# The last feed-forward block's gate and up products as seven block products instead of eight

## The chip, the cores and the metric

The kernel is one program on one core of a Trainium2 chip. The metric is the device time of one execution in microseconds (us), the median over several runs. The engines of the core are TensorE (PE in the rows: matrix products; PEld is its weight load), VectorE (DVE), ScalarE (ACT), GpSimd (POOL) and SyncE (SP), which issues the transfers of the weights.

## The reference

Two models run one after the other on 512 tokens of width 1024: two layers (a gated recurrent mixer, then banded attention, each with a memory attention and a feed-forward block), and a third with differential and forgetting attention. The change concerns the last feed-forward block, with D_MODEL = 1024 and D_FF_2 = 2816 = 22 tiles of 128 columns:

```python
h2 = rmsnorm_2(x, norm2_g[l])
g = jnp.einsum('bsd,df->bsf', h2, w_gate[l])
u = jnp.einsum('bsd,df->bsf', h2, w_up[l])
x = x + jnp.einsum('bsf,fd->bsd', jax.nn.silu(g) * u, w_down[l])
return rmsnorm_2(x, normf_g)
```

Everything is float32. After this block only the final norm is left.

## The kernel before

**Precision.** Each float32 operand of a large product is split in two fp32r parts: a high part (ScalarE copies it to fp32r) and a low part (VectorE subtracts the high one from the original). A product is three matmuls that accumulate in PSUM: high by high, high by low, low by high. Activations lie as [feature, token], so 512 tokens are the moving operand, and the stationary operand is a 128x128 piece of the weights.

**Weights.** All weights lie in the order of use in one array, cut in units of 2048 columns (1 MB; `UNITS`, made by `plan`). SyncE loads unit n into one of two `raw` buffers as soon as the low part of unit n-2 has been made. ScalarE makes `WH` (L1375) and VectorE `WL` (L1806), each in two pieces of 1024 columns, into two double buffers; a new one is begun when TensorE is through with the unit two before.

**One order for all engines.** `order` writes a list of steps; each engine goes through the same list and takes its part of each step, in order, and waits on semaphores. So a conversion that stands in the list behind another step waits for that step's work on the same engine. `conv_ahead` puts the conversions into the list.

**The last feed-forward block.** `ffn` runs two halves (`HALVES`: 12 and 10 of the 22 tiles). Per tile there are 8 K tiles x 3 = 24 matmuls for gate and 24 for up, all 128x128 by 512 tokens (step `fm`, L995). VectorE multiplies the gate by the row factor `Rsb` out of PSUM (L1768), ScalarE takes the silu (L1627), GpSimd multiplies by `Rsb` (L2383), VectorE multiplies by the up product (L2135), ScalarE and GpSimd split the result (L1642, L2391). After each half follow its down products (step `down`, L1299), in banks for four output tiles at a time, and VectorE adds them to X (L2160 and neighbours). The very last output tile is made in two token halves.

**Before the block.** The output projection of the attention makes the 8 tiles of X (L929, steps `out_rest` and `out_all`, tiles 4 to 7 with 24 matmuls each). For each tile the step `res_norm` follows: VectorE adds to X (L2106), ScalarE makes the scaled high part `hH` (L1609) and the square (L1617), VectorE the low part `hL` (L1774), GpSimd adds up the squares (L2374). After two tiles of the block, step `rstd_rows` sums over the partitions (L1080), ScalarE takes the root (L1426) and VectorE the reciprocal (L1842), which gives `Rsb`.

**At the end.** For the last four output tiles VectorE adds to X, ScalarE squares and scales (L1684, L1687), and VectorE adds the square to `acc` (L2171), in that order for each tile. Then the final norm follows.

## Time and profile before

| | us |
|---|---|
| median of 3 runs (lowest to highest) | 1824.84 (1824.78 to 1824.85) |
| profiled execution, span from first to last instruction | 1822.8 |
| a time of its own for the profiled execution, beside its span | none is given; the median of the runs is 2.0 above the span |
| TensorE busy | 1810.1 (99%) |
| TensorE weight loads | 1472.7 (81%) |
| VectorE busy | 938.6 (51%) |
| ScalarE busy | 727.8 (40%) |
| GpSimd busy | 272.3 (15%) |

The busy time of an engine counts every moment in which one of its instructions is open. Matmuls overlap in the pipeline, so the duration of one is longer than its share of the time: the share comes from the time that a row of many takes, divided by their count.

### The profile page before, as it was taken

The numbers are of one execution on the slowest core, as the hardware profiler recorded it, in microseconds if no ns is written. First come the engines' busy times: TensorE is split into PE (matmuls) and PEld (weight loads), VectorE is DVE, ScalarE is ACT, GpSimd is POOL, SyncE is SP. The second block draws the span as 40 slices with busy tenths as digits, with TensorE's granted clock in tenths as the row PEclk, the third lists the DMA queues.
The fourth block names the chain that finished last, engine by engine and source line by source line (L and its number), as shares of the span: only waits on it lengthen the run. The fifth ranks groups of instructions, "written<-read, shape, count | busy, mean of one in ns | idle before, by whom it ended". The sixth has DMA issues, their size and how long they took to land.

```text
span 1822.8 us, 21331 instructions
## 1 busy us (share of the span) xinstructions
PE 1810.1 (99%) x8733; PEld 1472.7 (81%) x8733; DVE 938.6 (51%) x1429; ACT 727.8 (40%) x1155; POOL 272.3 (15%) x241
## 2 busy tenths in 40 slices
PE   9999999999999999999999999999999999999998
PEld 7877788888888887878888888877777888888886
DVE  6878556443453456545653345458667443333324
ACT  5644444331332435654432233332567432212223
POOL 2001222210121200002221022103001222101210
PEclk9999999999999999999999999999999999999999
DMA  6121123222222333212223222232121132222221
GB/s 243 67 88 66 70 95 114 93 93 94 91 95 96 118 128 108 82 47 93 93 95 113 93 93 95 91 110 99 70 103 59 70 109 100 93 92 93 102 89 64
DMA packets 32337, 173.41 MB, mean 95 GB/s; under 512 B 4064, under 2 KB 6240, under 8 KB 14320
## 3 DMA queue, kind: packets, MB, share of 16 engines
q1 hardware_dynamic: 26848, 162.55, 25.0%
q10 hardware_dynamic: 5392, 9.51, 1.6%
q8 instruction: 69, 1.13, 0.2%
q14 instruction: 28, 0.23, 0.0%
HBM read 169.38 MB, written 2.13 MB: 94 GB/s over the span
## 4 chain that ended last, share of the span: by engine, by line
PE 96%; ACT 1%; DVE 1%; DMA 0%; POOL 0%; issue 0%; SPq 0%; ACTq 0%; DVEq 0%; POOLq 0%
PE ps L995 54%; PE ps L1299 20%; PE ps L929 7%; PE ps L1014 5%; PE ps L1141 2%; PE ps L1186 2%; PE ps L1166 2%; PE ps L1034 1%; PE ps L1225 1%; PE ps L1206 1%; DMA raw<-in_wall 0%; ACT PC L1543 0%; DVE WL L1806 0%; ACT WH L1375 0%; POOL sq L2326 0%
## 5 line engine op out<-in xcount | busy, mean ns | idle before, releaser
L995 PE MATMUL ps<-hH,WH 128*128 128x512 f32 x1456 | 570.9, 392 | 0.1
L1806 DVE TENSOR_TENSOR WL<-raw,WH 128x1024 fp32r<-128x1024 f32 (+2 forms) x308 | 377.3, 1264 | 368.1 <-ACT WH L1375 367.9
L995 PE MATMUL ps<-hH,WL 128*128 128x512 f32 x1456 | 566.7, 389 | 0.0
L995 PE MATMUL ps<-hL,WH 128*128 128x512 f32 x1456 | 566.7, 389 | 0.0
L1375 ACT ACTIVATE WH<-raw 128x1024 fp32r<-128x1024 f32 (+2 forms) x308 | 301.4, 1026 | 311.8 <-PE ps L1299 228.6
L995 PEld LDWEIGHTS ps<-hH,WH 128*128 128x128 f32 x1456 | 273.3, 188 | 65.3 <-issue 7.3
L995 PEld LDWEIGHTS ps<-hH,WL 128*128 128x128 f32 x1456 | 273.3, 188 | 57.0
L995 PEld LDWEIGHTS ps<-hL,WH 128*128 128x128 f32 x1456 | 273.3, 188 | 56.9 <-issue 1.0
L1299 PE MATMUL ps<-fL,WH 128*128 128x512 f32 x531 | 205.9, 388 | 0.0
L1299 PE MATMUL ps<-fH,WL 128*128 128x512 f32 x531 | 205.9, 388 | 0.0
L1299 PE MATMUL ps<-fH,WH 128*128 128x512 f32 x531 | 205.9, 388 | 0.0
L2383 POOL TENSOR_TENSOR Y<-Y,Rsb 128x512 f32<-128x512 f32 x66 | 85.2, 1292 | 544.0 <-ACT Y L1632 380.3
L1299 PEld LDWEIGHTS ps<-fH,WH 128*128 128x128 f32 x531 | 99.7, 188 | 20.6
L1299 PEld LDWEIGHTS ps<-fL,WH 128*128 128x128 f32 x531 | 99.7, 188 | 20.5
L1642 ACT ACTIVATE fH<-Z 128x512 fp32r<-128x512 f32 x66 | 41.7, 632 | 186.4 <-DVE Z L2135 186.4
L1299 PEld LDWEIGHTS ps<-fH,WL 128*128 128x128 f32 x531 | 99.7, 188 | 20.3
L2391 POOL TENSOR_TENSOR fL<-Z,fH 128x512 fp32r<-128x512 f32 x66 | 85.2, 1291 | 199.0 <-ACT fH L1642 199.0
L2135 DVE TENSOR_TENSOR Z<-ps,Y 128x512 f32<-128x512 f32 x66 | 45.3, 687 | 113.7 <-PE ps L995 108.9
L1768 DVE TENSOR_TENSOR GG<-ps,Rsb 128x512 f32<-128x512 f32 x66 | 45.4, 690 | 107.6 <-PE ps L995 107.6
L2124 DVE SCALAR_TENSOR_TENSOR Y<-GG,cols,Y 128x511 f32<-128x511 f32 x88 | 67.8, 770 | 40.4 <-ACT Y L1629 38.9
L1629 ACT ACTIVATE Y<-GG,cols 128x512 f32<-128x512 f32 x44 | 35.9, 815 | 111.1 <-DVE GG L1768 111.1
L1014 PE MATMUL ps<-WH,hH 128*128 128x256 f32 x256 | 73.5, 287 | 0.0
(369 smaller groups left out, 2020.7 us busy)
## 6 DMA issues: line engine op xcount, KB each, us to landing
raw<-in_wall SPq DMA_DIRECT2D x140, 1024.0 KB, 4.6
raw<-in_wall SPq DMA_DIRECT2D x12, 768.0 KB, 4.0
bias<-in_bias ACTq DMA_DIRECT2D x12, 256.0 KB, 3.3
X<-in_xt SPq DMA_DIRECT2D x8, 256.0 KB, 8.9
CB<-rows ACTq DMA_DIRECT2D x8, 256.0 KB, 3.3
raw<-in_wall SPq DMA_DIRECT2D x4, 256.0 KB, 5.8
mrA<-in_memt ACTq DMA_DIRECT2D x4, 256.0 KB, 6.3
Mb<-m_rows ACTq DMA_DIRECT2D x4, 256.0 KB, 4.8
```

Of the source, the lines that this page charges most:

```text
L929: mm = e.matmul(ps[b][:, :], ww[:, k, c:c + 128], x, start=(k == seq[0] and i == 0), stop=(k == seq[-1] and i == 2))
L995: mm = e.matmul(ps[b][:, 0:N], ww[:, k, c:c + 128], x[:, k, 0:N], start=(k == 0 and i == 0), stop=(k == 7 and i == 2))
L1014: mm = e.matmul(o, x[:, k, t * 128:t * 128 + 128], ww[:, k, :], start=(k == 0 and i == 0), stop=(k == 7 and i == 2))
L1299: mm = e.matmul(ps[b][:, t], ww[:, kx, mi * 128:mi * 128 + 128], x[:, k, t], start=(gi == first and kx == 0 and p == 0), stop=(gi == end a ...
L1375: e.activation(WH[n % NCV][:, c], raw[n % NRAW][:, c], ACT.Copy).then_inc(*mark("wh", n, x))
L1642: e.activation(F[i]["H"][:, k, :], F[i]["Z"][m % 2][:, :], ACT.Copy).then_inc(*mark("fH", i, int(half), k))
L1768: return e.tensor_tensor(dst, src, Rsb[:, :], ALU.mult)
L1806: e.tensor_tensor(WL[n % NCV][:, c], raw[n % NRAW][:, c], WH[n % NCV][:, c].bitcast(F32), ALU.subtract).then_inc(*mark("wl", n, x))
L2124: e.scalar_tensor_tensor(out=y[:, d:512], in0=gq[:, 0:512 - d], scalar=col(f"fw{i}", c), in1=y[:, d:512], op0=ALU.mult, op1=ALU.add).then_inc(
L2135: e.tensor_tensor(F[i]["Z"][m % 2][:, :], ps[BANK[(name, m)]][:, :], F[i]["Y"][m % 4][:, :], ALU.mult).then_inc(*mark("fz", name, m))
L2383: e.tensor_tensor(y[:, :], y[:, :], Rsb[:, :], ALU.mult).then_inc(*mark("fy", i, m))
L2391: e.tensor_tensor(F[i]["L"][:, k, :], F[i]["Z"][m % 2][:, :], F[i]["H"][:, k, :].bitcast(F32), ALU.subtract).then_inc(*mark("fL", i, int(h ...
```

## The change

The last block's gate and up products become one 2x2 block product, for each of 11 stages s of two gate tiles and two up tiles. The blocks of the weights are (gate, up) by (even K tiles, odd K tiles), 1024 columns each; the blocks of the activations are (even, odd K tiles) by (tokens 0 to 255, 256 to 511). Seven products q1 to q7, each of 4 K tiles x 2 column tiles x 3 = 24 matmuls of 256 tokens, take the place of eight. Their operands:

- Activations: the blocks themselves for q1, q2, q3 (`TH`, `TL`) and four sums for q4 to q7 (`DH`, `DL`). They are made in `res_norm`, for a pair of X tiles at a time, in one scratch tile `Tf`. The next pair's first scaling waits until the low parts of the pair before are done.
- Weights: the unit of conversion is now a chunk of 1024 columns, in one of four slots. For q5, q6, q3 and q7 VectorE first adds two blocks (or a sum and a block) into one of two `Wsum` buffers (step `wsum`); then ScalarE and VectorE convert it as any other (step `cconv`). A third `raw` buffer is used in the block.
- Results: q1, q6, q7, q4 accumulate in one bank, q5 and q3 in a second, q2 in a third. ScalarE copies the intermediate values out (step `wcopy`), VectorE combines them (`wc12`, `wc11`, `wz1`, `wz0`); gate factor, silu and GpSimd's two steps work on 1024 columns for two tiles at once.

The order of the products in a stage is q1, q5, q6, q3, q7, q2, q4, then down products of earlier tiles (24 matmuls of 512 tokens per piece: one piece in stages 1 and 2, two in stages 3 to 10). Stage 0 begins with q1, q5 and q2 over their first three K tiles, then `rstd_rows`, then their fourth. After stage 10 only four tiles of down products are left (`wtail`), so each of the last output tiles ends with 6 matmuls behind the others' where it was 9. The count of down matmuls is 528 before and after. The bytes loaded are the same.

```diff
+WINO = (2,)
+NSU = 11
+CHUNK = 1024
+W_SLOTS = 2 * NCV
...
+def down_pieces(s):
+    if s == 0:
+        return []
+    if s < 3:
+        return [(0, s - 1)]
+    return [((s - 1) // 2, 2 * ((s - 1) % 2) + x) for x in (0, 1)]
...
+def group_tiles(g):
+    return (0, 2) if g == 0 else (4 * g - 2, 4)
...
+def wino_sequence():
+    out = []
+    for s in range(NSU):
+        q = lambda n, p0=0, p1=4, s=s: ("q", s, n, p0, p1)
+        d = [("d",) + x for x in down_pieces(s)]
+        if s == 0:
+            out += [q(1, 0, 3), q(5, 0, 3), q(2, 0, 3), q(1, 3), q(5, 3), q(2, 3), q(6), q(3), q(7),
+                    ("q", 1, 1, 0, 4), q(4)]
+        elif s < 3:
+            out += ([] if s == 1 else [q(1)]) + [q(5), q(6), q(3), q(7), q(2), q(4)] + d
+        else:
+            out += [q(1), q(5), q(6), q(3), q(7), q(2), q(4)] + d
+    return out
...
+                else:
+                    c["sum"] = {5: ((units[0], CHUNK), (units[1], 0)), 6: ((i, "q", s, 5), (units[0], 0)),
+                                3: ((i, "q", s, 6), (units[1], CHUNK)), 7: ((units[0], 0), (units[0], CHUNK))}[q]
+                    c["place"] = {5: 0, 6: 1, 3: 0, 7: 1}[q]
+                c["from"] = units[0] if q == 1 else units[1]
...
     def conv_ahead(end):
-        while now["conv"] < min(end, len(UNITS)) and (now["conv"] < NCV or now["conv"] - NCV in done):
-            for x in (0, 1):
-                put("conv", now["conv"], x)
+        while now["conv"] < len(ITEMS):
+            item = ITEMS[now["conv"]]
+            kind, n = item
+            first = n if kind == "unit" else CHUNKS[n]["from"]
+            if first >= end or any((b if b[0] == "chunk" else b[1]) not in done for b in W_BEFORE[item]):
+                return
+            if kind == "unit":
+                for x in (0, 1):
+                    put("conv", n, x)
+            else:
+                for c in range(now["summed"], min(n + 2, len(CHUNKS))):
+                    if CHUNKS[c]["i"] == CHUNKS[n]["i"]:
+                        if CHUNKS[c]["sum"]:
+                            put("wsum", c)
+                        now["summed"] = c + 1
+                put("cconv", n)
             now["conv"] += 1
...
+        for at, x in enumerate(SEQUENCE):
+            conv_ahead(len(UNITS))
+            if x[0] == "d":
+                _, g, c = x
+                put("wd", i, g, c)
+                while late:
+                    put(*late.pop(0))
+                used((i, "d", g, c))
+                put("wx", i, g, c)
+                continue
+            _, s, q, p0, p1 = x
+            put("wp", i, s, q, p0, p1)
+            while late:
+                put(*late.pop(0))
+            if at == 2:
+                put("rstd_rows", FFN_NORMS[i], 61 if i == 2 else 60)
+            if p1 < 4:
+                continue
+            used((i, "q", s, q))
+            if q in (1, 5, 6, 7):
+                put("wcopy", i, s, q)
+            elif q == 3:
+                put("wc12", i, s)
+            elif q == 2:
+                put("wc11", i, s)
+            if q == (3 if s == 0 else 2):
+                put("wgate", i, s)
+            if q == 4:
+                put("wz1", i, s)
+                late.append(("wz0", i, s))
+        while late:
+            put(*late.pop(0))
+        hread = ("wq", i, NSU - 1, 4)
+        if i == 2:
+            put("sqrt_table")
+        for mg in (0, 1):
+            n = ROLE[i, "T", mg]
+            now["unit"] = n + 1
+            conv_ahead(n + 2)
+            for gi, ks in TAIL:
+                for mi in range(4):
+                    put("wtail", i, mg, gi, mi, n, ks)
+                    if gi == 2:
+                        put("res_ffn", i, 1, 4 * mg + mi, hread)
+            done.add(n)
+        if end:
+            rstd(end, 60)
     def ffn(i, acts, end):
...
+                elif what == "wp":
+                    i, st, pn, p0, p1 = a
+                    c = CHUNK_AT[i, "q", st, pn]
+                    kind = {1: "wA", 6: "wA", 7: "wA", 4: "wA", 5: "wD", 3: "wD", 2: "wB"}[pn]
+                    opens = pn in (1, 5, 2)
+                    if opens and p0 == 0:
+                        b, before = bank((kind, i, st), {"wA": ("wg", "z", 0), "wD": ("wg", "c12"), "wB": ("wg", "c11")}[kind] + (i, st),
+                                         hold=kind == "wA")
+                        if before:
+                            w.wait_ge(*at(*before))
+                    b = BANK[kind, i, st]
+                    if not opens:
+                        w.wait_ge(*at("wcopy", i, st, {6: 1, 7: 6, 4: 7, 3: 5}[pn]))
+                    w.wait_ge(*at("wl", "c", c))
+                    W = [x.rearrange("p (k c) -> p k c", k=4) for x in chunk_slot(c)]
+                    for p in range(p0, p1):
+                        w.wait_ge(*at("wg", "t", "L", i, p, int(pn > 3)))
+                        H, L = moving(pn, p)
+                        for u in (0, 1):
+                            for n, (ww, x) in enumerate(((W[0], H), (W[0], L), (W[1], H))):
+                                mm = e.matmul(ps[b][:, 256 * u:256 * u + 256], ww[:, p, 128 * u:128 * u + 128], x,
+                                              start=(opens and p == 0 and u == 0 and n == 0),
+                                              stop=(p == 3 and u == 1 and n == 2), skip_group_check=True)
+                    if p1 == 4:
+                        mm.then_inc(*mark("wq", i, st, pn))
+                        FREED["chunk", c] = ("wq", i, st, pn)
+                    if pn == 4:
+                        turns.append(b)
...
+                elif what == "wcopy":
+                    i, st, pn = a
+                    dst = {1: held_q1, 5: held_q5, 6: held_v, 7: held_w}[pn]
+                    w.wait_ge(*at("wq", i, st, pn))
+                    if st:
+                        w.wait_ge(*at(*{1: ("wg", "c11"), 5: ("wg", "z", "c22"), 6: ("wg", "c12"), 7: ("wg", "z", 1)}[pn], i, st - 1))
+                    e.activation(dst[:, :, :], by_tile(BANK["wD" if pn == 5 else "wA", i, st]), ACT.Copy).then_inc(
+                        *mark("wcopy", i, st, pn))
...
+                    if st in WINO_OF:
+                        i, p = WINO_OF[st], m // 2
+                        src = X[:, m, :].rearrange("p (h t) -> p h t", h=2)
+                        if p:
+                            w.wait_ge(*at("wg", "t", "L", i, p - 1, 1))
+                        e.activation(Tf[:, 1:3, :] if m % 2 else Tf[:, 0:8:7, :], src, ACT.Copy,
+                                     scale=col(st, m)).then_inc(*mark("wcopy", "t", "g", i, m))
+                        if m % 2:
+                            w.wait_ge(*at("wcopy", "t", "g", i, m))
+                            e.activation(TH[:, p, :, :], Tf[:, 0:3, :], ACT.Copy).then_inc(*mark("wcopy", "t", "H", i, p, 0))
+                            w.wait_ge(*at("wg", "t", "d", i, p, 4))
+                            e.activation(DH[:, p, :, :], Tf[:, 3:7, :], ACT.Copy).then_inc(*mark("wcopy", "t", "H", i, p, 1))
...
+                elif what == "wsum":
+                    c = CHUNKS[a[0]]
+                    src = []
+                    for y in c["sum"]:
+                        if len(y) == 2:
+                            w.wait_ge(*loaded(y[0]))
+                            src.append(raw[RAW_AT[y[0]]][:, y[1]:y[1] + CHUNK])
+                        else:
+                            w.wait_ge(*at("wg", "sum", CHUNK_AT[y]))
+                            src.append(Wsum[CHUNKS[CHUNK_AT[y]]["place"]][:, :])
+                    before = [v for v in range(a[0]) if CHUNKS[v]["sum"] and CHUNKS[v]["place"] == c["place"]]
+                    if before:
+                        w.wait_ge(*at("wl", "c", before[-1]))
+                    e.tensor_tensor(Wsum[c["place"]][:, :], src[0], src[1], ALU.add).then_inc(*mark("wg", "sum", a[0]))
...
+                    if st not in WINO_OF:
+                        low_part(st, m, col(st, m))
+                    elif m % 2:
+                        i, p = WINO_OF[st], m // 2
+                        B12 = Tf[:, 7:8, :].broadcast_to([128, 2, 256])
+                        w.wait_ge(*at("wcopy", "t", "g", i, m))
+                        e.tensor_tensor(Tf[:, 4:7:2, :], Tf[:, 0:3:2, :], B12, ALU.subtract).then_inc(
+                            *mark("wg", "t", "d", i, p, 2))
+                        w.wait_ge(*at("wg", "t", "d", i, p, 2))
+                        e.scalar_tensor_tensor(out=Tf[:, 5, :], in0=Tf[:, 0, :], scalar=-1.0, in1=Tf[:, 6, :],
+                                               op0=ALU.mult, op1=ALU.subtract).then_inc(*mark("wg", "t", "d", i, p, 3))
+                        w.wait_ge(*at("wg", "t", "d", i, p, 3))
+                        e.scalar_tensor_tensor(out=Tf[:, 3, :], in0=Tf[:, 5, :], scalar=-1.0, in1=Tf[:, 1, :],
+                                               op0=ALU.mult, op1=ALU.subtract).then_inc(*mark("wg", "t", "d", i, p, 4))
+                        w.wait_ge(*at("wcopy", "t", "H", i, p, 0))
+                        e.tensor_tensor(TL[:, p, :, :], Tf[:, 0:3, :], TH[:, p, :, :].bitcast(F32),
+                                        ALU.subtract).then_inc(*mark("wg", "t", "L", i, p, 0))
+                        w.wait_ge(*at("wcopy", "t", "H", i, p, 1))
+                        e.tensor_tensor(DL[:, p, :, :], Tf[:, 3:7, :], DH[:, p, :, :].bitcast(F32),
+                                        ALU.subtract).then_inc(*mark("wg", "t", "L", i, p, 1))
...
+                elif what == "wz1":
+                    i, st = a
+                    w.wait_ge(*at("wcopy", i, st, 7))
+                    w.wait_ge(*at("wcopy", i, st, 5))
+                    e.tensor_tensor(held_w[:, :, :], held_w[:, :, :], held_q5[:, :, :], ALU.add).then_inc(
+                        *mark("wg", "z", "c22", i, st))
+                    w.wait_ge(*at("wg", "z", "c22", i, st))
+                    w.wait_ge(*at("wpool", "y", i, st))
+                    e.scalar_tensor_tensor(out=yz[:, :, 256:512], in0=held_w[:, :, :], scalar=-1.0,
+                                           in1=yz[:, :, 256:512], op0=ALU.mult, op1=ALU.mult).then_inc(
+                        *mark("wg", "z", 1, i, st))
+                elif what == "wz0":
+                    i, st = a
+                    w.wait_ge(*at("wq", i, st, 4))
+                    w.wait_ge(*at("wpool", "y", i, st))
+                    e.scalar_tensor_tensor(out=yz[:, :, 0:256], in0=by_tile(BANK["wA", i, st]), scalar=-1.0,
+                                           in1=yz[:, :, 0:256], op0=ALU.mult, op1=ALU.mult).then_inc(
+                        *mark("wg", "z", 0, i, st))
...
+                elif what == "wgate":
+                    i, st = a
+                    R = Rsb[:, :].rearrange("p (o t) -> p o t", o=1).broadcast_to([128, 2, 512])
+                    w.wait_ge(*at("wsilu", i, st))
+                    e.tensor_tensor(yz[:, :, :], yz[:, :, :], R, ALU.mult).then_inc(*mark("wpool", "y", i, st))
+                elif what == "wz0":
+                    i, st = a
+                    f = 2 * st % 8
+                    w.wait_ge(*at("wsilu", "H", i, st))
+                    e.tensor_tensor(FL[:, f:f + 2, :], yz[:, :, :], FH[:, f:f + 2, :].bitcast(F32),
+                                    ALU.subtract).then_inc(*mark("wpool", "L", i, st))
```

## Rows read from the trace of the kernel before

**Rows 1.** The page: busy time per engine (part 1) and the chain's shares (part 4)

```profile
PE 1810.1 (99%) x8733; PEld 1472.7 (81%) x8733; DVE 938.6 (51%) x1429; ACT 727.8 (40%) x1155; POOL 272.3 (15%) x241
...
PE 96%; ACT 1%; DVE 1%; DMA 0%; POOL 0%; issue 0%; SPq 0%; ACTq 0%; DVEq 0%; POOLq 0%
```

**Rows 2.** Windows: stretch, length, busy us (count) by engine, clock, DMA share, GB/s

```profile
1463.00:1582.70 119.70, 119.70 (x530) 99.07 (x529) 47.32 (x46) 37.36 (x47) 29.67 (x23) 1.00 0.27 97
```

**Rows 3.** The chain in order of time, last block: start us, us, what

```profile
1451.26 10.88 PE ps L995 x48
...
1463.00 119.73 PE ps L995 x528
...
1648.01 108.80 PE ps L995 x480
```

**Rows 4.** The same chain, 256-column matmuls of a memory product

```profile
676.20 5.76 PE ps L1014 x48
```

**Rows 5.** Timeline of TensorE, 256-column matmuls with weights stationary: start, us

```profile
12.47 0.28 PE L958 MATMUL ps<-mLA,WH 128*128 128x256 f32 x1
12.58 0.28 PE L958 MATMUL ps<-mHA,WL 128*128 128x256 f32 x1
```

**Rows 6.** VectorE's groups by shape, 1451 to 1823: count, busy us, mean ns, idle before

```profile
L1806 DVE TENSOR_TENSOR WL<-raw,WH 128x1024 fp32r<-128x1024 f32 x58 | 73.3, 1303 | 75.6 <-ACT WH L1375 75.6
...
L2160 DVE TENSOR_TENSOR X<-X,ps 128x512 f32<-128x512 f32 x15 | 10.2, 685 | 12.1 <-PE ps L1299 12.1
...
L1842 DVE RECIPROCAL Rsb<-Rsb 128x512 f32<-128x512 f32 x1 | 3.4, 3353 | 4.7 <-ACT Rsb L1426 4.7
...
L2287 DVE SCALAR_TENSOR_TENSOR X<-X,cols,ps 128x256 f32<-128x256 f32 x2 | 0.9, 471 | 0.0
```

**Rows 7.** ScalarE's groups by shape, the same stretch

```profile
L1375 ACT ACTIVATE WH<-raw 128x1024 fp32r<-128x1024 f32 x58 | 57.9, 1046 | 60.2 <-PE ps L1299 58.6 <-POOL acc L2374 1.6
...
L1609 ACT ACTIVATE hH<-X,cols 128x512 fp32r<-128x512 f32 x2 | 1.4, 724 | 3.3 <-DVE X L2106 3.3
```

**Rows 8.** GpSimd's groups by shape, the same stretch

```profile
L2383 POOL TENSOR_TENSOR Y<-Y,Rsb 128x512 f32<-128x512 f32 x22 | 28.4, 1293 | 163.7 <-ACT Y L1627 163.7
L2374 POOL TENSOR_TENSOR acc<-acc,sq 128x512 f32<-128x512 f32 x2 | 2.7, 1337 | 5.0 <-ACT sq L1617 5.0
```

**Rows 9.** Timeline of VectorE ahead of the block and in it: start, us, idle before

```profile
1430.20 0.68 DVE L2106 TENSOR_TENSOR X<-X,ps 128x512 f32<-128x512 f32 x1
...
1456.67 2.36 DVE L1806 TENSOR_TENSOR WL<-raw,WH 128x1024 fp32r<-128x1024 f32 x2 [2.52 <-ACT WH L1375]
...
1476.31 2.60 DVE L1806 TENSOR_TENSOR WL<-raw,WH 128x1024 fp32r<-128x1024 f32 x2 [1.65 <-ACT WH L1375]
```

**Rows 10.** Timeline of GpSimd beside it

```profile
1475.40 1.29 POOL L2391 TENSOR_TENSOR fL<-Z,fH 128x512 fp32r<-128x512 f32 x1 [0.47 <-ACT fH L1642]
```

**Rows 11.** Timeline of VectorE at 1272 us, then of GpSimd there

```profile
1272.62 3.45 DVE L1806 TENSOR_TENSOR WL<-raw,WH 128x1024 fp32r<-128x1024 f32 x2
```
```profile
1272.13 1.73 POOL L2413 TENSOR_TENSOR dk<-U,RC 128x512 f32<-128x512 f32 x1 [2.15 <-DVE U L1769]
```

**Rows 12.** Windows after TensorE's last matmul: columns as in rows 2

```profile
1816.00:1817.00 1.00, 0.00 (x0) 0.00 (x0) 1.00 (x3) 0.00 (x0) 0.00 (x0) 0.75 1.06 373
1817.00:1818.00 1.00, 0.00 (x0) 0.00 (x0) 1.00 (x2) 0.00 (x0) 0.00 (x0) 0.50 0.59 209
```

**Rows 13.** Timeline of VectorE at the end of the down products

```profile
1805.13 0.69 DVE L2160 TENSOR_TENSOR X<-X,ps 128x512 f32<-128x512 f32 x1 [1.35 <-PE ps L1299]
1806.51 0.69 DVE L2171 TENSOR_TENSOR acc<-acc,sq 128x512 f32<-128x512 f32 x1 [0.70 <-ACT sq L1684]
1807.17 0.69 DVE L2160 TENSOR_TENSOR X<-X,ps 128x512 f32<-128x512 f32 x1
...
1810.69 0.68 DVE L2156 TENSOR_TENSOR acc<-acc,sq 128x512 f32<-128x512 f32 x1
```

**Rows 14.** Transfers issued from 1400 to 1480: count, KB each, us to landing

```profile
raw<-in_wall SPq DMA_DIRECT2D x7, 1024.0 KB, 4.5
```

375 lines of the change are left out of this document (339 added, 36 removed).

## The prediction

> **What bounds the kernel now.** I read the page first: TensorE is busy for 1810.1 of 1822.8 us and makes 96% of the chain that ends last; VectorE is at 51%, ScalarE at 40%, GpSimd at 15% [rows 1]. Then a window of the last block: TensorE has no idle time in 119.70 us while VectorE is busy for 47.32 and GpSimd for 29.67 [rows 2]. So only two things can move the time: what a TensorE instruction costs, and a wait that TensorE does not have today. The price of a matmul comes from the chain, not from the duration of one, since they overlap: 119.73 us for 528 and 108.80 for 480 are 226.7 ns for each matmul of 512 columns, and with the first 48 the gate and up products are 1056 matmuls, 239.4 us [rows 3].
>
> **The matmuls.** The change makes 11 x 7 x 24 = 1848 matmuls of 256 columns of them. A row of 48 such matmuls takes 5.76 us, 120.0 ns each [rows 4], and where the weights are the stationary operand, as here, they start 0.11 to 0.12 us apart [rows 5]. So 221.8 us take the place of 239.4: 17.6 us less. Seven eighths of 239.4 would be 29.9 less; the difference is that 256 columns cost 6.7 ns more than half of 512 (226.7 / 2 = 113.3). The 528 down matmuls stay at 226.7 ns: nothing. The Trainium skill, "TensorE: Matmul & The Clock Gate", section "Back-to-back issue gap", gives an isolated spacing of N / 2.4 + 2.5 ns, 109 and 216; an estimate by it would be 228 - 202 = 26 us saved. The rows do not agree for this data type, and the sum goes by the rows.
>
> **VectorE in a stage.** The extra work is on VectorE. A low part of 1024 columns costs 1.18 us (2.36 for two in a row [rows 9]; the mean duration, 1303 ns, holds waits on ScalarE and contention [rows 6]); the trace has no sum of two weight blocks, but it is an operation of the same kind and size, so I take 1.18 (bounds: that, and the mean of 1.30, 0.5 us a stage more). A stage from the third on has 4 sums and 9 low parts (15.3), the gate factor on 1024 columns (1.2), five combining passes of 512 columns at 0.69 (3.4), and four adds to X at 0.69 (2.8) [rows 6]: 22.7 us. GpSimd's two passes double in width, 2.6 us each by two of 1293 ns [rows 8], and they slow VectorE: two low parts took 2.60 where the GpSimd row overlaps them by 0.38 us, against 2.36, a loss of 0.24 or 0.63 of the overlap [rows 9, 10]; at 1272 us an overlap of 1.24 made them 3.45, a loss of 0.88 of it [rows 11]. So 5.2 us cost 3.3 (up to 4.6), and the stage asks VectorE for 26.0. TensorE takes 7 x 2.88 + 2 x 5.44 = 31.0, so this is hidden, with four converted chunks (8.6 us of products) as the cushion. In stage 0, without down products, it is 20.9 against 20.2, and in stages 1 and 2 24.8 against 25.6: covered by the cushion only. ScalarE has 11 passes of 1024 columns at 1.05 and 4 of 512 at about 0.7, 14 us a stage [rows 7]: nothing. Loads of 1 MB land 4.5 us after their issue [rows 14]. The later of a stage's two units can be issued when q4's low part of the stage before is made, some 9 us after that stage's q1 began, and its first sum stands 17 us after it: over 3 us to spare, nothing; were it gone, VectorE's cushion of 8.6 would still lie before TensorE. The wait of the products on the copies of earlier ones lies one product (2.88 us) behind a copy of 0.7: nothing. The last stage's product parts, sign passes, high and low part take about 8.5 us after q4; two down pieces and the first tail tiles are 16 us of work: nothing.
>
> The Trainium skill, "GPSIMD Engine Reference", section "Specifications", says that GpSimd's SBUF interfaces are shared with VectorE, with contention where a VectorE instruction has two SBUF inputs. The trace agrees (the 0.63 and 0.88 above); all of the new sums and low parts are of that kind.
>
> **The entry.** Here I see new waits. The four pairs of X tiles go through one scratch tile, so they run one after the other. From the end of a pair's last low part to the end of the next one's: add to X 0.7; scale, square, scale on ScalarE 1.9 (three passes of at most 0.72 [rows 7], overlapping a little); the first difference 0.65, with 0.45 for GpSimd's square sum (1337 ns [rows 8]) beside it; two dependent differences of 256 columns, 0.47 each [rows 6]; the high part of four blocks 1.05; their low part 1.2, with 0.5 for the next square sum; six handovers, 0.25. That is 7.6 us. The first add stands at 1430.20 [rows 9] and does not move. Pair 0 needs about 7.0, to 1437.2. In pair 1 the conversion of the last output unit stands between its two tiles, 2.0 on ScalarE and half of 2.36 behind it and its first one's handover, 3.8 in all: to 1448.6. Pair 2: to 1456.2. Now `conv_ahead` has put q5's sum and q1's low part, 2.3: q1 can start at 1458.5, and TensorE was free at 1451.26 [rows 3]. Pair 3: to 1466.1. The conversion of q5 stands behind it in the list, since its second unit is past the end given to `conv_ahead`: 1.1, so q5 starts at 1467.2.
>
> TensorE has then worked for 2.2 of 15.9 us. The granted clock falls when it idles: 0.75 and then 0.50 in the two windows after its last work [rows 12]. At half the clock 18 matmuls of q5 take 4.3 us and not 2.2; I take this once, to 1471.5 (bounds: none, or q2 as well, 2 more). q2 was ready at 1469.5 and ends at 1473.7, the row sums at 1474.6 (0.86 between two rows [rows 3]). Then the root, 0.7, and the reciprocal, 3.35 [rows 6], block VectorE until 1478.7; behind it wait the sum for q7 and the low part of q3, 2.3. So q3 starts at 1481.0; TensorE alone (fourth K tiles 2.2, q6 2.9) would have been there at 1479.6. Without any wait q3 would start 8.64 + 0.86 + 2.88 after 1451.26, at 1463.6. The entry costs 17.4 us. From there I followed the list to stage 2: the chunk behind the first silu is ready about 0.1 us before TensorE needs it, later ones 1 to 5 us before: no further wait.
>
> **The end.** For the last tiles, add, square and sum follow each other for each tile, and come 2.04 us apart (1805.13 to 1807.17 [rows 13]), as do 9 matmuls of 226.7 ns. Now a tile has 6, 1.36 us. VectorE keeps its 2.04 for two tiles and then has the last sum of squares (at 1810.69 [rows 13]) behind the end of TensorE: the last matmul comes 4.2 instead of 6.2 us after the first of these adds, and the chain behind it does not: 2.0 us.
>
> **The sum.** The profiled span is 1822.8, 2.0 below the median of the runs, and I keep that. 1822.8 - 17.6 + 17.4 + 2.0 = 1824.6 of span, 1826.6 us of time.
>
> **The rivals.**
> - *VectorE falls behind in the stages.* For it: stages 0 to 2 have no margin, and the second silu product waits in VectorE's queue for GpSimd, up to 3 us in which nothing else is done. With 0.88 of the overlap lost the three stages ask for 74.6 against TensorE's 71.4, 3 us, and a wait in each adds 1 to 3: 5 to 12 us. It decides when VectorE's work and waits in stages 0 to 2 pass 71.4 + 8.6. Against it: from stage 3 on there are 5 us to spare in each. Time 1831 to 1839.
> - *The entry is short.* The pairs overlap more, contention with GpSimd is less (4 x 0.95), the clock comes back at once (2.1): 6 us less; if moreover the reciprocal hides, 8. Time 1818 to 1821. This is the side of a gain. It decides when q3 starts before 1475.6. For it: each term of 7.6 is a chain of parts that I priced at full duration. Against it: all four pairs share one scratch tile.
> - *A 256-column matmul costs half of a 512-column one* (113.3 ns by the rows' own halves): 30 us saved and not 17.6, time 1814. Against it are both rows of 256 columns. The spacing rule named above is of this kind.
> - *The clock stays low longer,* over q5, q2 and the row sums: 3 us more, 1829 to 1831. The rows show no matmul at half clock, so the length is open.
>
> **How the numbers follow.** My forecast's own range, for errors of half a microsecond in each pair and the two bounds of the clock, is 1822 to 1830, chance 0.50. VectorE behind: 0.22. Short entry: 0.15. Half price: 0.03. Low clock: 0.10. A difference of 0.2%, 3.65 us, is about what a measurement of this kernel can tell from no change: below 1821.2 is faster, above 1828.5 slower. Faster: nearly all of the short entry and the half price, 0.17. Of the forecast, 0.38 lie within and 0.12 above; the two others are slower: 0.43 in all, with a little of the low clock and the rest within: 0.40. The range 1817 to 1837 leaves out the half price and the far end of VectorE behind.
>
> **What would show it.** Right: spacing of 120 ns within the new products; TensorE idle from 1451.3 for 7 us, again before q5, and 1 us before the fifth product, with VectorE's low part named as releaser; no idle from stage 1 to the tail; the final sums waiting on VectorE for 2 us. Wrong: a first product without a wait before it, a low clock for more than one product, or TensorE waiting on low parts in every stage.

## The result, and the profile after

The changed kernel takes 1837.82 us (median of 4 runs, 1836.91 to 1840.12), the kernel before 1824.81 in the same series: ratio 1.0074, 95% interval [1.0059, 1.0088]. It is 13 us slower. The median lies 11.2 above the 1826.6 forecast, 0.8 beyond the range's upper end, and inside the rival "VectorE falls behind in the stages" (1831 to 1839). The profiled execution took 1838.41, with a span of 1836.7: 13.9 more than before.

The page, parts 1 and 4:

```profile
PE 1800.8 (98%) x9522; PEld 1501.5 (82%) x9522; DVE 1105.8 (60%) x1570; ACT 788.4 (43%) x1216; POOL 277.2 (15%) x219
...
PE 89%; DVE 5%; ACT 3%; DMA 1%; issue 1%; POOL 0%; SPq 0%; ACTq 0%; DVEq 0%; POOLq 0%
```

TensorE is busy 9.3 us less than in [rows 1], and the span is 13.9 longer. So TensorE stands idle for some 23 us that were not there, and its share of the chain fell from 96 to 89%. Windows show where (columns as in [rows 2]):

```profile
1561.34:1823.00 261.66, 261.66 (x1758) 242.99 (x1758) 206.40 (x192) 113.26 (x131) 45.19 (x16) 1.00 0.27 93
...
1451.26:1486.00 34.74, 22.41 (x136) 20.99 (x136) 26.87 (x25) 18.48 (x22) 4.86 (x3) 0.75 0.11 31
...
1584.03:1615.09 31.06, 31.06 (x218) 29.16 (x218) 25.76 (x24) 13.26 (x15) 5.76 (x3) 1.00 0.30 102
```

From 1561.34 on there is no idle time for 261.66 us. All that is lost lies before, in the entry and the first three stages. The third row is one stage in the steady state: 31.06 us, as forecast (31.0), in which VectorE is busy for 25.76 (forecast 26.0). All of TensorE's waits in that first stretch, from its timeline:

```profile
1458.12 0.55 PE L1644 MATMUL ps<-TH,WH 128*128 128x256 f32 x1 [5.75 <-issue]
...
1467.42 0.55 PE L1644 MATMUL ps<-DH,WH 128*128 128x256 f32 x1 [5.13 <-DVE WL L2281]
...
1482.00 0.35 PE L1644 MATMUL ps<-TH,WH 128*128 128x256 f32 x1 [1.45 <-DVE WL L2281]
...
1493.40 0.39 PE L1644 MATMUL ps<-DH,WH 128*128 128x256 f32 x1 [2.54 <-ACT held L1788]
...
1505.05 0.38 PE L1644 MATMUL ps<-TH,WH 128*128 128x256 f32 x1 [1.27 <-ACT held L1788]
...
1529.78 0.39 PE L1644 MATMUL ps<-DH,WH 128*128 128x256 f32 x1 [1.73 <-ACT held L1788]
...
1533.45 0.38 PE L1644 MATMUL ps<-TH,WH 128*128 128x256 f32 x1 [0.55 <-ACT held L1788]
...
1557.66 0.39 PE L1644 MATMUL ps<-DH,WH 128*128 128x256 f32 x1 [1.21 <-ACT held L1788]
...
1561.34 0.39 PE L1644 MATMUL ps<-TH,WH 128*128 128x256 f32 x1 [0.54 <-ACT held L1788]
```

The first three are the forecast's waits, within 1.0 us of its times (1458.5, 1467.2, 1481.0): q1, q5, q3 of stage 0. The other six were not in it: q4 of stage 0, q3 of stage 1, then q6 and q3 of stages 2 and 3. Their releaser is a ScalarE copy of an earlier product (`wcopy`), 7.84 us in all.

TensorE waits 7.84 us, but loses more than that: in the first product behind each wait some 0.25 us, and once the clock. After the wait of 2.54 the granted clock fell (0.51 from 1494 to 1496), and the three products from 1493.40 on took 10.38 us, not 8.64: 1.74 more. The same stretches in windows: these three products with the wait behind them, then all from q3 of stage 0 to q3 of stage 3, in which VectorE is busy for 65.18 of 79.34 us:

```profile
1493.40:1505.05 11.65, 10.38 (x72) 10.18 (x72) 9.79 (x9) 5.09 (x7) 1.41 (x2) 0.85 0.26 91
...
1482.00:1561.34 79.34, 71.50 (x529) 68.37 (x529) 65.18 (x61) 35.09 (x42) 14.32 (x6) 0.98 0.28 94
```

The account. A product of stage 3 and later takes 2.879 us and a down piece 5.455 (20.15 for 168 matmuls and 10.91 for 48 in the chain, below). Between q3 of stage 0 and q3 of stage 3 lie 20 products and two pieces, 68.5 us; measured 1561.34 - 1482.00 = 79.3, so 10.8 are lost there (7.84 of waits, 1.74 of clock, 1.2 behind the waits). q3 starts 18.4 after the 1463.6 of no wait. From the start of the last down matmul to the end of the span it is 13.7 us (1822.99 to 1836.7), against 11.8 before (1811.04 to 1822.8): 2.0 with the decimals kept. The matmuls: 1848 at 119.9 ns, and 528 down matmuls at 227.3 ns where 226.7 was taken: 17.5 less. -17.5 + 18.4 + 10.8 + 2.0 = 13.7, of 13.9 measured.

```profile
1584.03 20.15 PE ps L1644 x168
1604.18 10.91 PE ps L1667 x48
```

Now the place of the first unforeseen wait. ScalarE's timeline, then VectorE's, then GpSimd's:

```profile
1490.86 1.06 ACT L1797 ACTIVATE yz<-gs 128x1024 f32<-128x1024 f32 x1 [5.36 <-DVE gs L2307]
1491.82 1.04 ACT L1780 ACTIVATE WH<-Wsum 128x1024 fp32r<-128x1024 f32 x1
1492.77 0.58 ACT L1788 ACTIVATE held<-ps 128x512 f32<-128x512 f32 x1
```
```profile
1486.51 1.22 DVE L2275 TENSOR_TENSOR Wsum<-raw,raw 128x1024 f32<-128x1024 f32 x1 [1.69 <-issue]
1487.65 1.22 DVE L2281 TENSOR_TENSOR WL<-raw,WH 128x1024 fp32r<-128x1024 f32 x1
1488.78 0.68 DVE L2289 TENSOR_TENSOR gs<-ps,held 128x512 f32<-128x512 f32 x1
1489.60 1.23 DVE L2307 TENSOR_TENSOR gs<-gs,Rsb 128x1024 f32<-128x1024 f32 x1
1490.74 1.22 DVE L2275 TENSOR_TENSOR Wsum<-Wsum,raw 128x1024 f32<-128x1024 f32 x1
1492.89 2.55 DVE L2281 TENSOR_TENSOR WL<-Wsum,WH 128x1024 fp32r<-128x1024 f32 x1 [0.93 <-ACT WH L1780]
```
```profile
1491.99 2.37 POOL L2957 TENSOR_TENSOR yz<-yz,Rsb 128x1024 f32<-128x1024 f32 x1 [25.80 <-ACT yz L1797]
```

Read backwards from 1493.40: q4 waits for the copy of q7 (1492.77), whose product had ended some 4.8 us before it: the next one, q1 of stage 1, starts at 1487.82. That copy stands in ScalarE's queue behind the conversion of a sum (1491.82) and the silu (1490.86), and the silu waits 5.36 us for VectorE's gate factor (1489.60). VectorE reaches the gate factor late: it had the sum for stage 1's q5 in its queue ahead of it, which waited 1.69 us. The row names no releaser; the fourth buffer below takes this wait away, so it was for the load. And the sum's low part (1492.89) takes 2.55 us beside GpSimd's product.

### The profile page after: what moved, and what is told of

It is laid out like the page before. It is cut to its first block, busy times and chain, and to the rows that moved or that the text cites. A ratio compares the mean times of both kernels' runs of the same rounds, so it can differ in the third digit from the quotient of the medians.

```text
span 1836.7 us, 23157 instructions
## 1 busy us (share of the span) xinstructions
PE 1800.8 (98%) x9522; PEld 1501.5 (82%) x9522; DVE 1105.8 (60%) x1570; ACT 788.4 (43%) x1216; POOL 277.2 (15%) x219
## 3 DMA queue, kind: packets, MB, share of 16 engines
HBM read 169.38 MB, written 2.13 MB: 93 GB/s over the span
## 4 chain that ended last, share of the span: by engine, by line
PE 89%; DVE 5%; ACT 3%; DMA 1%; issue 1%; POOL 0%; SPq 0%; ACTq 0%; DVEq 0%; POOLq 0%
PE ps L1311 40%; PE ps L1615 13%; PE ps L1644 9%; PE ps L1245 6%; PE ps L1330 5%; PE ps L1667 5%; PE ps L1457 2%; PE ps L1502 2%; PE ps L1482 2%; DMA raw<-in_wall 1%; DVE WL L2281 1%; PE ps L1350 1%; PE ps L1693 1%; PE ps L1541 1%; DVE Wsum L2275 1%
## 5 line engine op out<-in xcount | busy, mean ns | idle before, releaser
L2259 DVE TENSOR_TENSOR WL<-raw,WH 128x1024 fp32r<-128x1024 f32 (+2 forms) x244 | 299.8, 1268 | 277.4 <-ACT WH L1769 277.3
L1311 PE MATMUL ps<-hH,WH 128*128 128x512 f32 x1104 | 433.7, 393 | 0.1
L1311 PE MATMUL ps<-hH,WL 128*128 128x512 f32 x1104 | 429.8, 389 | 0.0
L1311 PE MATMUL ps<-hL,WH 128*128 128x512 f32 x1104 | 429.8, 389 | 0.0
L1644 PE MATMUL ps<-DH,WH 128*128 128x256 f32 x352 | 101.5, 288 | 10.6 <-ACT held L1788 5.5
L1644 PE MATMUL ps<-DL,WH 128*128 128x256 f32 x352 | 101.1, 287 | 0.0
L1644 PE MATMUL ps<-DH,WL 128*128 128x256 f32 x352 | 101.1, 287 | 0.0
L2281 DVE TENSOR_TENSOR WL<-raw,WH 128x1024 fp32r<-128x1024 f32 x51 | 72.8, 1428 | 41.3 <-ACT WH L1780 41.0
L1644 PE MATMUL ps<-TH,WH 128*128 128x256 f32 x264 | 76.9, 291 | 9.6 <-issue 5.7
L1644 PEld LDWEIGHTS ps<-DH,WH 128*128 128x128 f32 x352 | 69.1, 196 | 11.5 <-ACT held L1788 6.1
L1615 PEld LDWEIGHTS ps<-fL,WH 128*128 128x128 f32 x352 | 66.1, 188 | 13.7
L1615 PEld LDWEIGHTS ps<-fH,WH 128*128 128x128 f32 x352 | 66.1, 188 | 13.7
```

Source lines behind the costliest of these rows:

```text
L1311: mm = e.matmul(ps[b][:, 0:N], ww[:, k, c:c + 128], x[:, k, 0:N], start=(k == 0 and i == 0), stop=(k == 7 and i == 2))
L1615: mm = e.matmul(ps[b][:, t], ww[:, kx, mi * 128:mi * 128 + 128], x[:, k, t], start=(gi == first and kx == 0 and p == 0), stop=(gi == end a ...
L1644: mm = e.matmul(ps[b][:, 256 * u:256 * u + 256], ww[:, p, 128 * u:128 * u + 128], x, start=(opens and p == 0 and u == 0 and n == 0), stop= ...
L2259: e.tensor_tensor(WL[v][:, c], raw[RAW_AT[n]][:, c], WH[v][:, c].bitcast(F32), ALU.subtract).then_inc(*mark("wl", n, x))
L2281: e.tensor_tensor(L, chunk_src(c), H.bitcast(F32), ALU.subtract).then_inc(*mark("wl", "c", c))
```

## The experiments

Each compared with the kernel before on the same chip. "q3" is where q3 of stage 0 starts in the trace, and "lost behind" what is lost from there to q3 of stage 3, as worked out above (measured distance less 68.5). The medians are of 4 to 11 runs, of 2 for GpSimd's product and for the sum without the second unit.

How far the two kinds of number carry. Of the single edits only that of ten narrow sums has an interval clear of the change's, [1.0059, 1.0088]. What is said of the others rests on "lost behind", which is 10.2 to 10.8 in the change and in the three versions whose edit touches only the entry or the tail. q3 itself starts anywhere from 1480.57 to 1482.00 in the seven traces whose entry is the change's own, with a granted clock of 0.53 to 0.74 from 1467 to 1474, so a shift of up to 1.4 us there says nothing. One more term differs between executions: TensorE is idle for about 2 us before the small matmuls of the final norm, and in five of the profiled executions (fourth buffer, GpSimd's product, second unit, filling, ten sums) four of these took 0.85 us and in the change's 0.46, at a granted clock of 0.50 (1820.44 to 1825.06 in the fourth buffer's trace) and of 1.00. That adds 1.8 us to the span. From the chains of the two:

```profile
1821.42 0.85 PE ps L1372 x4
...
1825.93 0.46 PE ps L1369 x4
```

| kernel | median us | ratio to before, 95% | q3 | lost behind |
|---|---|---|---|---|
| the change | 1837.82 | 1.0074 [1.0059, 1.0088] | 1482.00 | 10.8 |
| fourth raw buffer | 1835.32 | 1.0056 [1.0041, 1.0071] | 1481.32 | 6.6 |
| conversions ahead at the entry | 1837.45 | 1.0069 [1.0052, 1.0086] | 1481.16 | 10.7 |
| tail in two parts | 1835.5 | 1.0060 [1.0045, 1.0075] | 1480.77 | 10.2 |
| these three together | 1830.32 | 1.0035 [1.0022, 1.0048] | 1481.33 | 6.4 |
| GpSimd's product narrow | 1834.77 | 1.0056 [1.0036, 1.0076] | 1481.45 | 6.4 |
| sum without the second unit | 1835.71 | 1.0061 [1.0041, 1.0081] | 1481.49 | 6.6 |
| filling matmuls | 1836.54 | 1.0066 [1.0051, 1.0081] | 1479.54 | 10.3 |
| gate step later | 1838.19 | 1.0076 [1.0059, 1.0093] | 1480.57 | 9.9 |
| high part later | 1838.94 | 1.0078 [1.0065, 1.0090] | 1481.55 | 10.0 |
| ten sums narrow | 1830.59 | 1.0034 [1.0022, 1.0046] | 1480.81 | 4.4 |
| combined, five edits | 1826.62 | 1.0012 [1.0003, 1.0020] | 1480.57 | 2.6 |
| combined, six edits | 1826.20 | 1.0009 [1.0000, 1.0018] | 1480.31 | 2.2 |
| reciprocal later, entry's own order | 1826.28 | 1.0008 [0.9999, 1.0017] | 1477.52 | 4.6 |
| reciprocal later, conversions ahead | 1827.12 | 1.0013 [1.0005, 1.0022] | 1478.45 | 4.6 |

**Fourth raw buffer.** The loads of stage s+1's second unit no longer wait for the slot of stage s's.

```diff
-    free, held, loads = [-2, -1, 0], [None] * 3, [0] * 3
+    free, held, loads = [-2, -1, 0, 0], [None] * 4, [0] * 4
...
+        raw.append(place("raw3", [128, SLOT], offset=raw3_at))
```

> A fourth raw buffer in the block (in the 8 KB of acc, sq and diag, which are idle between the row sums and the tail); nothing else changes. Theory L (the load loop): VectorE waits for the second unit of stages 1 to 3 because its buffer is given back only two products before its first sum, and everything behind it in the lists, ScalarE's copies of the products above all, comes late. Then the waits of 1.7, 3.1 and 4.7 us on VectorE go, most of the 10.8 us that TensorE loses between its fifth product and 1561 us go with them, and the time falls by 6 to 10 us, to 1828 to 1832. Rival C (capacity): VectorE has too much work in stages 0 to 3 together with GpSimd's contention, and its waits for loads were slack; then the time falls by 3 us at most. Both leave the entry as it is (fifth product at about 1482).

Measured: 2.5 us less in the medians, 4.2 less lost behind q3. VectorE's waits for loads are gone (in the change 1.69, 3.06 and 2.86; the 4.7 of the expectation is the last load's own time, not the wait). The median is within what the capacity rival gave (3 at most) and far from the 6 to 10 of theory L. So the loads have a part, but not most of it. What remains is one large wait, at q3 of stage 1, and again a copy behind a ScalarE step that waits for VectorE; TensorE, ScalarE, VectorE:

```profile
1502.60 0.38 PE L1647 MATMUL ps<-TH,WH 128*128 128x256 f32 x1 [2.77 <-ACT held L1791]
```
```profile
1501.01 1.06 ACT L1816 ACTIVATE FH<-yz 128x1024 fp32r<-128x1024 f32 x1 [3.20 <-DVE yz L2339]
1501.97 0.58 ACT L1791 ACTIVATE held<-ps 128x512 f32<-128x512 f32 x1
```
```profile
1500.23 0.68 DVE L2339 SCALAR_TENSOR_TENSOR yz<-ps,yz 128x512 f32<-128x512 f32 x1
```

**Conversions ahead at the entry.** q5 and q2 are converted before the last pair of X tiles.

```diff
                 if c:
                     done.add(n)
+                    if stage == "C":
+                        conv_ahead(n + 3)
```

> Only the order of the list at the entry changes: q1's conversion stands ahead of the X tile 5 step, and those of q5, q2 and q6 with their sums ahead of the X tile 7 step. VectorE's work is the same. Theory E (the entry is a matter of order: TensorE idles because the conversions stand behind the last pair): q1 starts 2 us earlier, q5 starts 5 to 6 us earlier, the last pair is ready about 3.5 us later, and the fifth product starts 3 to 6 us earlier, 1832 to 1835 in all. Rival (the entry is a matter of VectorE's total work): the fifth product starts within 1 us of where it did, no change in the time.

Measured: q5 starts at 1461.61, 5.8 us earlier, but the row sums then wait for GpSimd's sum of squares (1472.62 in that trace), and q3 starts where it did. In that wait of 5.16 us the clock fell, too: the granted clock is 0.50 from 1472 to 1478, and the 42 matmuls from 1473.68 to q3 take 7.5 us and not 5.0. The gain went into the next wait and the clock behind it.

**Tail in two parts.** In the second half of the tail, each output tile ends with 9 matmuls behind the others' and not 6.

```diff
-TAIL = ((0, (0,)), (1, (1,)), (2, (2, 3)))
+TAILS = (((0, (0,)), (1, (1,)), (2, (2, 3))), ((1, (0,)), (2, (1, 2, 3))))
```

> The tail of the last four output tiles in two parts of 3 and 9 matmuls in place of 3, 3 and 6, so that 9 stand between the last tiles as in the kernel before. Theory T (the end lost 2 us because the tile step of VectorE and ScalarE, 2.04 us, is longer than 6 matmuls): 2.0 us less, the distance from TensorE's last down matmul to the end goes from 13.6 back to 11.5 us. Rival (the end is late for another reason): no change.

Measured: 2.3 us less in the medians, and in the traces the distance from q3 of stage 3 to the end of the span falls from 275.4 to 273.4: the size that the forecast gave the end.

**The three together.**

> The fourth buffer, the entry order and the tail together. If each works as its theory says the gains add up to 11 to 16 us, 1822 to 1827; if the load loop was only a symptom of the late entry, the sum is smaller than that of the parts.

Measured: 7.5 us less than the change (11 to 16 expected), still 0.35% slower than before. Lost behind q3 are 6.4, about as with the buffer alone; and the final norm's matmuls ran at the full clock, which they did not in the buffer's trace.

**GpSimd's product narrow.** Its multiplication by `Rsb` covers 16 of 512 columns of each tile; the output is not the reference's.

```diff
-                    e.tensor_tensor(yz[:, :, :], yz[:, :, :], R, ALU.mult)
+                    e.tensor_tensor(yz[:, :, 0:16], yz[:, :, 0:16], R[:, :, 0:16], ALU.mult)
```

> GpSimd's multiplication by the row factor covers 16 of each 512 columns, so it leaves most of that product out; nothing else changes. Rival C (capacity and contention on VectorE): the low part beside it falls from 2.55 to 1.2 us, and the time falls by 3 to 5 us. Theory L (the load loop): the silu chain is 2.3 us shorter, but VectorE then waits for the loads that much longer; 0 to 2 us less.

Measured: 3.1 less in the medians, 4.4 less lost behind q3, and the low part beside it takes 1.23 and not 2.55: contention and the length of the chain silu, product, combination cost about as much as the loads. The run does not part the two.

**Sum without the second unit.** The sum for q5 takes its second operand from the first unit, so it does not wait for the second; the output is not the reference's.

```diff
-5: ((units[0], CHUNK), (units[1], 0))
+5: ((units[0], CHUNK), (units[0], 0))
```

> The sum for q5 reads its second block from the first unit in place of the second one, so that no sum waits for the second unit at that place; the products are then not those of the reference. Count, size and place of all operations are the same. Theory L: VectorE's waits for loads go or move to the sum for q3, two sums later, and the time falls about as with the fourth buffer, 5 to 10 us. Rival C: 3 us at most.

Measured: as the fourth buffer, 6.6 lost behind q3, and the same waits within 0.2 us of their places. Both take the load's wait away in different ways and leave the same rest.

**Filling matmuls.** 58 and 60 bf16 matmuls before q1 and q5 of stage 0 keep TensorE working.

```diff
+                        if st == 0 and pn in WARM:
+                            for _ in range(WARM[pn]):
+                                e.matmul(ps[b][:, 0:256], KB[:, 0, :], KB[:, 0:2, :], start=True, stop=True)
```

> Before q1 and before q5 of stage 0 TensorE runs 58 and 60 bf16 matmuls of 256 columns on constants, into the bank that the product opens next. Theory K (the clock had its own price at the entry: 36 matmuls of q5 and q2 took 7.25 us and not 4.3): the granted clock stays at 1.0 through the entry, the fifth product starts 1.5 to 3 us earlier, and the time falls by 2 to 4 us. Rival (the clock's price is hidden behind VectorE's work): the fifth product starts as before and the time does not change.

Measured: the granted clock is 1.00 from 1451.26 to 1486 (0.75 in the change), q3 starts at 1479.54, 1.0 to 2.5 earlier than in the seven traces with the change's own entry, and the medians differ by 1.3. The low clock at the entry was worth 1 to 2.5 us.

**Gate step later.** Stage 0's gate factor and silu stand behind the copy of q7.

```diff
-            if q == (3 if s == 0 else 2):
+            if q == (7 if s == 0 else 2):
```

> In stage 0 the gate step (factor, silu, GpSimd's product) stands behind q7 and its copy in the list, and not behind q3. Theory S (the wait of 2.5 us before q4 of stage 0 comes from ScalarE, whose copy of q7 stood behind a silu that waited for VectorE): the wait goes, the clock does not fall there, and the time falls by 2 to 4 us. Rival (the product would wait for a low part at the same place anyway): within 1 us.

Measured: q4 starts without a wait, and one of 3.89 stands at q3 of stage 1 in its place, with the granted clock at 0.50 behind it (from 1502.36 to 1507.65). No change in time.

**High part later.** ScalarE's `wz0` step (and GpSimd's) stands behind the copy of the next q5.

```diff
+                while split and q == 5:
+                    put(*split.pop(0))
...
-                elif what == "wz0":
+                elif what == "wfh":
```

> The changed kernel, with one step moved: ScalarE's high part of the gated product (and GpSimd's low part behind it) stands in the list behind ScalarE's copy of the next stage's q5 and not ahead of it. The work of every engine is the same. Theory Q (the copies stand in ScalarE's in-order queue behind a step that waits for VectorE): the waits at the heads of stages 1, 2 and 3 (1.27, 1.73 + 0.55 and 1.21 + 0.54 us) go, with some of the clock's loss: 3 to 5 us less than the changed kernel, 1833 to 1835; the wait of 2.54 before q4 of stage 0, which has the silu before it and not this step, stays. Rival V (VectorE has too much work there, so a wait only moves to the next low part): 0 to 1 us less, 1837 to 1838, and TensorE's waits name VectorE's low parts.

Measured: 1.1 above the change, with intervals that overlap: no gain. My theory Q, that the order of ScalarE's queue is the cause, fails when tried alone. Rival V has the time, but not its sign: the waits still name ScalarE's copies, not low parts. The wait of 1.27 at stage 1 is gone, those at q6 of stages 2 and 3 have shrunk from 1.73 and 1.21 to 0.58 and 0.56, and those at q3 of the same stages have grown from 0.55 and 0.54 to 2.13 and 2.12:

```profile
1492.24 0.39 PE L1647 MATMUL ps<-DH,WH 128*128 128x256 f32 x1 [1.83 <-ACT held L1791]
...
1531.19 0.39 PE L1647 MATMUL ps<-TH,WH 128*128 128x256 f32 x1 [2.13 <-ACT held L1791]
...
1560.02 0.39 PE L1647 MATMUL ps<-TH,WH 128*128 128x256 f32 x1 [2.12 <-ACT held L1791]
```

**Ten sums narrow.** VectorE has 12 us less to do up to stage 2; orders, loads and conversions are as they were. The output is not the reference's.

```diff
-                    e.tensor_tensor(Wsum[c["place"]][:, :], src[0], src[1], ALU.add).then_inc(*mark("wg", "sum", a[0]))
+                    few = bool(before) and c["key"][2] < 3
+                    e.tensor_tensor(*(x[:, 0:16] if few else x[:, :] for x in (Wsum[c["place"]], src[0], src[1])),
+                                    ALU.add).then_inc(*mark("wg", "sum", a[0]))
```

> The changed kernel, with ten of the sums of weight blocks in stages 0 to 2 (those for q3 and q7 of stage 0, all four in stages 1 and 2) made over 16 of their 1024 columns, so the output is not the reference's. VectorE's work falls by 10 x 1.2 = 12 us up to stage 2; queues, loads and the work of the others stay. Theory V (VectorE's amount of work sets the waits after the fifth product): 6 to 10 us less, 1828 to 1832. Rival L (the loads of each stage's second unit set them): the sum for q5 still waits for its load, 2 to 4 us less, 1834 to 1836. Rival Q (order alone): 1 to 3 us less.

Measured: 7.2 less in the medians, and 6.4 less lost behind q3 in the trace: the largest effect of a single edit, and that of theory V. VectorE's waits for loads are still there (1.26, 3.19 and 2.74), so it is the work that was taken away. Some 1.7 of the 6.4 are the clock, which does not fall behind the shorter waits. The waits of stage 2 are gone, and the first two are smaller; at stage 3, whose sums are whole again, 1.09 and 0.54 stand (1.21 and 0.54 in the change). The two that are smaller:

```profile
1490.72 0.39 PE L1644 MATMUL ps<-DH,WH 128*128 128x256 f32 x1 [1.04 <-ACT held L1788]
...
1500.28 0.39 PE L1644 MATMUL ps<-TH,WH 128*128 128x256 f32 x1 [0.68 <-ACT held L1788]
```

**Combined, five edits**: the three above, the filling matmuls, and the high part later.

> All that is kept of the earlier edits: fourth raw buffer, conversions of q5 and q2 ahead of the last pair, tail in two parts, 58 and 60 filling matmuls before q1 and q5, and the high part of the gated product behind the copy of q5. The output is the reference's. If theory Q holds, the 2.78 us before stage 1's third product goes with its clock loss: 1830.3 less 3 to 5 for that and less 0 to 1.5 for the clock at the entry: 1825 to 1827, level with the kernel before. If the waits only move: 1829 to 1830.5.

Measured: 1826.62. The same move of the high part that gave nothing alone goes with 3.7 us here, together with the filling matmuls (1.3 alone): by difference some 2.4 are its own. No run has the three and the high part without the filling, so this is a difference and not a test. Lost behind q3 fall from 6.4 to 2.6, by 3.8: the wait at q3 of stage 1 (2.78) is gone, and the clock no longer falls there. It speaks for this: once the loads no longer hold VectorE up, the order of the queue counts.

**Combined, six edits**: the gate step later too.

> As the one before it, with the gate step of stage 0 behind the copy of q7 too. The 0.76 us wait before q4 of stage 0 goes if the order of ScalarE's queue sets it: 0.5 to 1 us less than without. Where VectorE's work sets it, the later silu makes GpSimd's product and the combining passes later, and a wait of the same size or more stands in stage 1: no less, or up to 2 us more.

Measured: 0.4 less, not told apart from it. The 0.75 before q4 is gone, and the wait at q7 of stage 1 has grown from 0.87 to 1.22. Two waits of any size are left from the row sums on:

```profile
1480.31 0.35 PE L1656 MATMUL ps<-TH,WH 128*128 128x256 f32 x1 [1.44 <-DVE WL L2293]
...
1502.16 0.39 PE L1656 MATMUL ps<-DH,WH 128*128 128x256 f32 x1 [1.22 <-ACT held L1800]
```

**Reciprocal later**, in both orders of the entry. VectorE's reciprocal stands just ahead of the gate step.

```diff
+                if s == 0:
+                    put("rrow_late", FFN_NORMS[i])
                 put("wgate", i, s)
```

> The fourth raw buffer, the two-part tail, the filling matmuls, the moved high part and the moved gate step, but the conversions at the entry in their own order, and VectorE's reciprocal moved behind the low parts of q3 and q7, just ahead of the gate step. The output is the reference's. Theory E (the entry costs what its list costs: q5 at 1467.3, row sums at 1471.8, fourth K tiles and q6 after them): q3 starts at 1477.8, 2.5 us before the 1480.3 of the version before it, no low part ahead of it, and the time is 1 to 2.5 less than 1826.2: 1823.7 to 1825.2. Rival V (VectorE's work up to stage 2 is what counts, and the 3.35 us are only paid later): the wait reappears in stages 0 and 1 and the time is 1825.7 to 1827.

> As the one before it, with the conversions of q5 and q2 ahead of the last pair of X tiles. Row sums at 1472.8 as then (GpSimd's sum), fourth K tiles 2.2 and q6 2.9 behind: q3 at 1479.0 instead of 1480.3 by theory E, 0.5 to 1.3 less than 1826.2. By rival V, no less than 1826.

Measured: 1826.28 and 1827.12, no less. q3 starts at 1477.52 (theory E: 1477.8) without a wait, 2.8 earlier than in the version with six edits, and 2.4 more are lost behind it. TensorE, then VectorE:

```profile
1493.83 0.36 PE L1656 MATMUL ps<-DH,WH 128*128 128x256 f32 x1 [1.75 <-DVE WL L2293]
```
```profile
1484.43 3.35 DVE L2394 RECIPROCAL Rsb<-Rsb 128x512 f32<-128x512 f32 x1
```

The earlier start was right and worth nothing: the 3.35 us are paid later. The wait stood before q3 of stage 0 (1480.31) and stands now before q6 of stage 1 (1493.83), the sixth product from there. That is Rival V in its time and its mechanism; it had put the wait in stages 0 and 1, and it is in stage 1 alone.

## Why the prediction was wrong

**The matmuls** were right: 119.9 ns for 120.0, 17.5 saved for 17.6.

**The entry** was right in each place within 1.0 us, and in its sum: 18.4 for 17.4. The 36 matmuls of q5 and q2 took 7.25 us for 6.5: 18 at the low clock cost 3.8 and not 4.3, but it lasted until about 1473.5. Here two errors of the working partly cancel.

**VectorE in a stage** was right in its sum (25.76 busy for 26.0), and so was the steady state.

**The end** was right: 2.0 for 2.0, and splitting the tail otherwise gave 2.3 back.

**The step that failed** is the last sentence of the entry, "no further wait", and behind it the cushion of "four converted chunks (8.6 us of products)" that was to cover stages 0 to 2. The forecast had itself put q3 behind its own low part, with TensorE 1.4 us early. A product that waits for its low part says that VectorE is not ahead by anything: the cushion is nil at that moment. From there to stage 2 its work and waits come straight onto TensorE's path: 10.8 us. Ten narrow sums (12 us of VectorE's work) took 6.4 of the 10.8 away; a fourth buffer or a sum without its load 4.2; a narrow GpSimd product 4.4; all six edits together 8.6. These overlap, so they are not added. Part of it is the clock: the forecast has it fall only at the entry, and it fell again behind the wait of 2.54, for 1.74 us. Without the 10.8 the time would have been 1827.0, beside 1826.6 forecast; that it comes so close owes something to luck, as the two errors at the entry show.

Three smaller errors lie inside it. I gave the load of the second unit "over 3 us to spare"; VectorE waited for one in each of stages 0 to 2, as here ahead of stage 3's q5 (1.69 at stage 0's):

```profile
1541.87 1.23 DVE L2275 TENSOR_TENSOR Wsum<-raw,raw 128x1024 f32<-128x1024 f32 x1 [2.86 <-DMA raw<-in_wall]
```

I had put the first sum 17 us after q1 of the stage before. Up to stage 2 it stands in the list behind q7, at about 14.4, two products (5.8 us) behind the release of the slot, and the load takes 4.7 of them. The release itself is VectorE's work: in stage 2 it came 14.9 us after q1 (1522.14 to 1537.07) and not 9, since VectorE was late. So a late VectorE makes the load late, and the load VectorE. The chain shows it:

```profile
1535.82 1.24 DVE WL L2281
...
1537.07 4.72 DMA raw<-in_wall
```

The other two. I gave the copies a margin of one product (2.88) against 0.7 and left out what stands ahead of them in ScalarE's queue: silu and high part, which wait for VectorE. And GpSimd's cost to VectorE was taken as a sum over a stage; in stage 0 it falls on one low part (1.22 becomes 2.55) for which the rest of the queue waited.

**The rival** "VectorE falls behind in the stages" was right in its place and its price: 5 to 12 for 10.8. Its condition, VectorE's work and waits in stages 0 to 2 above 80.0 us, I have not measured as such; from q3 of stage 0 to q3 of stage 3 VectorE is busy for 65.2 of 79.3 us and waits in most of the rest, 7.6 us for loads and 6.0 for ScalarE's conversions. So it is not work alone that fills the time, but a queue in which work and waits stand one behind the other. The sign that I gave for it was TensorE waiting on low parts; the trace names ScalarE's copies, one step further along the chain. Its chance, 0.22, was too low for what the working showed. Against it I had the 5 us to spare from stage 3 on, which is so, and comes too late.

**Where the gain went.** With all edits, time is level with before (1.0008 [0.9999, 1.0017]); no version was faster. There the matmuls save 17.5, and q3 starts 13.9 to 16.7 later than it could; in the change the chain up to q5 runs through the sums and differences of the X tiles, which are made pair by pair first. For the version with six edits the account is 1822.8 - 17.5 + 16.7 + 2.2 = 1824.2 of span, measured 1824.4. So the entry is the larger loss, and the forecast had it; the 10.8 behind it are what it missed. What would bring q3 forward meets VectorE's work: 21.9 of 24 us busy from 1476 to 1500 in the version with the late reciprocal. A shorter chain of pairs, with a second scratch tile, was not tried.

## What to carry to other kernels

A cushion of prepared work counts only where the trace, or the forecast's own times, show the preparing engine ahead. If the consumer waits for it once, follow the producer's whole queue from that moment, with the loads that it waits for, until the surplus of the later stages has made up for it. And before a wait is "fixed" by order alone, ask what the engine behind it is busy with: four edits of order here (entry, gate step, high part, reciprocal) moved a wait, and none of them gained anything, the first three alone, the last on top of the others. And look at the clock behind each wait: here a wait of 2.5 us cost another 1.7.
